# The opening of a two-layer transformer kernel: four phases against one stage with hand-ordered engines

## The reference, cut to what matters

```python
h, hc = x, ctx
mod  = jnp.split((silu_c  @ w_mod[l] + b_mod[l])[:, None, :], 6, axis=-1)   # 1024 -> 6 x 1024
modc = jnp.split( silu_cc @ w_mod[l] + b_mod[l], 6, axis=-1)
u  = modulate(rmsnorm(h,  g_mix_pre[l]), mod[0],  mod[1])     # x * (1 + scale) + shift
uc = modulate(rmsnorm(hc, g_mix_pre[l]), modc[0], modc[1])
t = mixer_inputs(jnp.split(u  @ w_in, IN_OFFSETS, axis=-1), ...)
s = mixer_inputs(jnp.split(uc @ w_in, IN_OFFSETS, axis=-1), ...)
```

## Time and profile before

| | us |
|---|---|
| median of 3 runs (lowest to highest) | 3320.12 (3318.76 to 3322.37) |
| profiled execution | 3324.58 |
| its span, first to last instruction | 3322.8 |
| TensorE busy in it | 3188.5 (96%) |
| DVE, ACT, GpSimd busy | 1708.6, 1135.9, 208.4 |
| mean granted clock of TensorE | 0.983 |

### The profile page before, as it was taken

The page is one execution under the profiler, slowest core; times in us unless marked ns, Lnnn a source line. Parts: engine busy times, 40 slices in busy tenths (PEclk is TensorE's granted clock), DMA queues, the critical chain, the costliest instruction groups (busy, mean ns, idle before and its releaser), DMA issues. The chain is left out here.

```text
span 3322.8 us, 46746 instructions
## 1 busy us (share of the span) xinstructions
PE 3188.5 (96%) x18520; PEld 2889.8 (87%) x18520; DVE 1708.6 (51%) x3172; ACT 1135.9 (34%) x1931; POOL 208.4 (6%) x170
## 2 busy tenths in 40 slices
PE   7999999999999999899999999999999999899999
PEld 4999988998899789899999988887887787788887
DVE  6644445424357865664222475545534478555333
ACT  3223334433322544221222432334433325442223
POOL 0001100100021011000000000110100110100000
PEclk8999999999999999899999989999999999989999
DMA  6511320231052123442221443141221421443333
GB/s 207 174 39 58 83 95 27 77 102 39 26 184 77 39 73 125 133 127 65 69 63 52 142 151 108 60 127 39 99 79 39 159 89 39 140 140 99 106 86 103
DMA packets 352211, 310.42 MB, mean 93 GB/s; under 512 B 40510, under 2 KB 329228, under 8 KB 350604
## 3 DMA queue, kind: packets, MB, share of 16 engines
q1 hardware_dynamic: 330894, 240.65, 24.1%
q10 hardware_dynamic: 21118, 67.03, 5.5%
HBM read 273.94 MB, written 33.29 MB: 92 GB/s over the span
## 5 line engine op out<-in xcount | busy, mean ns | idle before, releaser
L923 PE MATMUL ps<-u_hi,w_hi 128*128 128x384 f32 (+1 forms) x2080 | 602.3, 352 | 25.0 <-DVE u_lo L2521 8.5
L923 PE MATMUL ps<-u_lo,w_hi 128*128 128x384 f32 (+1 forms) x2080 | 596.6, 349 | 0.0
L923 PE MATMUL ps<-u_hi,w_lo 128*128 128x384 f32 (+1 forms) x2080 | 596.6, 349 | 0.0
L2133 DVE TENSOR_TENSOR w_lo<-w_raw,w_hi 128x2048 fp32r<-128x2048 f32 x129 | 297.4, 2305 | 359.5 <-ACT w_hi L1586 357.7
L923 PEld LDWEIGHTS ps<-u_hi,w_hi 128*128 128x128 f32 x2080 | 379.0, 189 | 48.0 <-issue 22.0
L923 PEld LDWEIGHTS ps<-u_hi,w_lo 128*128 128x128 f32 x2080 | 382.3, 189 | 18.8
L923 PEld LDWEIGHTS ps<-u_lo,w_hi 128*128 128x128 f32 x2080 | 382.0, 189 | 18.3
L1586 ACT ACTIVATE w_hi<-w_raw 128x2048 fp32r<-128x2048 f32 x129 | 246.1, 1908 | 198.2 <-issue 90.3
L1301 PE MATMUL ps<-u_hi,w_hi 128*128 128x384 f32 (+1 forms) x816 | 306.1, 375 | 5.9 <-ACT space L1895 3.8
L1301 PE MATMUL ps<-u_hi,w_lo 128*128 128x384 f32 (+1 forms) x816 | 296.5, 363 | 0.0
L1301 PE MATMUL ps<-u_lo,w_hi 128*128 128x384 f32 (+1 forms) x816 | 293.9, 360 | 0.0
(11 more groups left out here) (303 smaller groups left out, 5153.8 us busy)
## 6 DMA issues: line engine op xcount, KB each, us to landing
w_raw<-in_w_in SPq DMA_DIRECT2D x288, 256.0 KB, 4.1
space<-in_w_mod SPq DMA_DIRECT2D x48, 1024.0 KB, 5.4
w_raw<-in_w_gate_up SPq DMA_DIRECT2D x176, 256.0 KB, 4.1
w_raw<-in_w_down SPq DMA_DIRECT2D x114, 192.0 KB, 2.9
w_raw<-in_w_branch SPq DMA_DIRECT2D x64, 256.0 KB, 3.5
w_raw<-in_w_out SPq DMA_DIRECT2D x48, 256.0 KB, 3.7
m_scratch<-space ACTq DMA_DIRECT2D x3, 3072.0 KB, 9.8
space<-m_scratch ACTq DMA_DIRECT2D x3, 3072.0 KB, 10.4
```

Of the source, the lines that this page charges most:

```text
L923: last = nc.tensor.matmul(ps[:, 2 * (t % 2) + b, 0:a1 - a0], wv[w][:, k, j * P:(j + 1) * P], xx[:, k, a0:a1], start=(k == 0 and w == 0 and ...
L2133: V.tensor_tensor(w_lo[slot][:, :], w_raw[slot][:, :], w_hi[slot][:, :].bitcast(F32), ALU.subtract).then_inc(w_lo_done, 1)
```

## The change

The four opening phases become one phase, `opening`, in which each engine has a list of its own and no meeting stands until its end; TensorE counts itself out (`end_products`) before its last two chunks.

- SP: the tokens come first, then the modulation units in the order 0, 4, 1, 5, 2, 6, 3, 7, each as two DMAs; `w_raw0` stands after unit 1; then layer 1's vectors, `w_raw1` and the small broadcasts. The first background units now wait for the store of the tokens (`h_stored`) too.
- ACT squares the tokens token-major from `x_tok` with `accum_out`, so the sums of squares come without DVE and TensorE; it copies the lower half of each turned token tile, DVE the upper.
- DVE scales all eight chunks by the spread root into `first_x` as soon as the root is there; the gain is no longer in it. A pair of modulation units (p and p + 4) gives shift and gain of two chunks (`pair`), and with them ACT finishes a chunk (`chunk`: two Identity passes with scale and bias, then `u_hi`).
- The low part is made by DVE for chunks 0, 2, 4, 6, 7 and by GpSimd for 1, 3, 5.
- The products with the first weight unit (`first_chunk`) are interleaved with the modulation products. `MOD_DVE` is now (5, 6).
- The store of the tokens moves from the head of `norm_mix` to the end of ACT's list; the two rope tables are loaded in the opening. The lambda factors (`head_factors`) move behind it, into the `gemm` phase.

The tables, the plan and SP's list:

```diff
-MOD_DVE = (2, 4)
-MOD_PE = (0, 1, 3, 5, 6, 7)
+MOD_LOADS = (0, 4, 1, 5, 2, 6, 3, 7)
+MOD_DVE = (5, 6)
+MOD_PE = (0, 4, 1, 2, 3, 7)
...
-    phases = [("setup", 0, None), ("load_x", 0, None), ("mod", 0, None)]
+    phases = []
...
-            phases.append(("norm_mix", l, None))
+            phases.append(("opening", l, None))
...
+            for i in MOD_LOADS:
+                for j in range(2):
+                    sp.dma_start(mod_ring[i].rearrange("p (k n) -> p k n", k=KD)[:, 4 * j:4 * j + 4, :],
+                                 mod_cols(0, i * 256)[:, 4 * j:4 * j + 4, :]).then_inc(mod_landed[i], 16)
+                if i == 1:
+                    load_unit(groups_in_order[0], 0, 0)
             load_vectors(sp, 1)
+            load_unit(groups_in_order[1], 0, 0)
...
-                            if phases[index - 1][0] == "close":
+                            if phases[index - 1][0] in ("opening", "close"):
                                 sp.wait_ge(h_stored, 16 * stored)
```

TensorE's list:

```diff
+            def opening(g):
+
+                pe.wait_ge(consts_made, 1)
+                for t in range(NT):
+                    turn_tokens(t)
+                    if t == 4:
+                        turn_vectors(0)
+                pe.wait_ge(scalars_in, 1)
+                mod_product(0, 0)
+                first_roots()
+                mod_product(0, 1)
+                mod_product(1, 0)
+                mod_columns(0, 0)
+                mod_product(1, 1)
+                mod_product(2, 0)
+                mod_columns(1, 0)
+                mod_product(2, 1)
+                mod_columns(2, 1)
+                first_chunk(g, 0)
+                first_chunk(g, 1)
+                mod_product(3, 0)
+                mod_product(3, 1)
+                summed_columns(0, 1)
+                mod_product(4, 0)
+                mod_columns(3, 2)
+                mod_product(4, 1)
+                mod_product(5, 0)
+                mod_columns(4, 2)
+                mod_product(5, 1)
+                first_chunk(g, 2)
+                summed_columns(1, 2)
+                first_chunk(g, 3)
+                mod_columns(5, 3)
+                turn_vectors(1)
+                first_chunk(g, 4)
+                first_chunk(g, 5)
+                ph.end_products(True)
+                first_chunk(g, 6)
+                first_chunk(g, 7)
```

On ACT a chunk, the squares, the order of its list, and the store with its place before:

```diff
+                def chunk(k):
+                    act.wait_ge(x_scaled, k + 1)
+                    act.wait_ge(pair_made, k // 2 + 1)
+                    for sg, seg in segments(False):
+                        last = A(first_x[:, k, seg], first_x[:, k, seg], ACT.Identity, bias=mod_t[:, 0, k, sg:sg + 1],
+                                 scale=gain[:, 0, 0, k, sg:sg + 1])
+                    last.then_inc(first_full, 1)
+                    act.wait_ge(first_full, k + 1)
+                    A(u_hi[:, k, :], first_x[:, k, :], ACT.Copy).then_inc(first_high, 1)
...
+                    A(token_square, x_tok[:, t, :], ACT.Square, accum_out=mean[:, t:t + 1]).then_inc(tokens_squared, 1)
...
+                row(0)
+                row(1)
+                act.wait_ge(w_landed[0], 64)
+                A(w_hi[0][:, :], w_raw[0][:, :], ACT.Copy).then_inc(w_hi_done, 1)
+                row(2)
+                chunk(0)
+                chunk(1)
+                row(3)
+                chunk(2)
+                chunk(3)
+                row(4)
+                row(5)
...
+                chunk(4)
+                chunk(5)
+                chunk(6)
+                split(following, 0, 0)
+                chunk(7)
+                act.wait_ge(vec_turned, 2)
+                A(vec[:, 1, :], ps[:, 4, 0:N_ROWS], ACT.Copy).then_inc(vec_copied, 1)
+                act.dma_start(h_dram[:, :, :], space[:, 8:16, :]).then_inc(h_stored, 16)
...
-                act.dma_start(h_dram[:, :, :], space[:, 8:16, :]).then_inc(h_stored, 16)
```

On DVE the scaling behind the spread root and what follows it, and GpSimd's low parts:

```diff
+                for k in range(KD):
+                    V.tensor_tensor(two(first_x[:, k, :], False), tile_at(8 + k, False), ps[:, 6:8, 0:TOK // 2],
+                                    ALU.mult).then_inc(x_scaled, 1)
+                dve.wait_ge(vec_copied, 1)
+                pair(0, 2)
+                dve.wait_ge(w_hi_done, 1)
+                V.tensor_tensor(w_lo[0][:, :], w_raw[0][:, :], w_hi[0][:, :].bitcast(F32),
+                                ALU.subtract).then_inc(w_lo_done, 1)
+                low(0)
+                sums(0)
+                pair(1, 4)
+                sums(1, 2)
+                pair(2, 7)
+                pair(3, 8)
+                low(4)
+                low(6)
+                split(following, 0, 0)
+                dve.wait_ge(first_low[1], 3)
+                low(7)
+                scalars()
...
+                    for k in (1, 3, 5):
+                        pool.wait_ge(first_high, k + 1)
+                        G.tensor_tensor(u_lo[:, k, :], first_x[:, k, :], u_hi[:, k, :].bitcast(F32),
+                                        ALU.subtract).then_inc(first_low[1], 1)
```

More of the change, by code:

```diff
@@ L564, in norm_spec @@
         def norm_spec(kind, l):
-            if kind == "norm_mix":
-                return [(list(range(8, 16)), KD, False, lambda k, s: gain[:, l, 0, k, s:s + 1],
-                         lambda k, s: mod_t[:, l, k, s:s + 1], (u_hi, u_lo), FFN_SCR)]
             return [(list(range(0, 8)), KD, True, None, None, 8, FFN_SCR)]
@@ L889, in mod_product @@
+            def mod_product(at, half):
+                i = MOD_PE[at]
+                if half == 0 and at < 3:
+                    pe.wait_ge(x_copied[at % 2], NT - 1 + at // 2)
+                if half == 0 and at > 3:
+                    pe.wait_ge(x_scaled, KD)
+                pe.wait_ge(mod_landed[i], 16 * 2)
+                for k in range(4 * half, 4 * half + 4):
+                    last = nc.tensor.matmul(ps[0:2, MOD_BANK[at], 0:256], silu_c[:, k, :],
                                             mod_ring[i][:, k * 256:(k + 1) * 256], start=k == 0, stop=k == KD - 1)
-                last.then_inc(row_ready, 1)
@@ new lines, in summed_columns, with first_chunk @@
+            def summed_columns(at, pair):
+                pe.wait_ge(first_summed, at + 1)
+                pe.wait_ge(pair_made, pair)
+                for j in range(2):
+                    last = part_product(first_part[:, at], j, 4 * MOD_DVE[at], 5)
+                last.then_inc(columns_made, 1)
+            def first_chunk(g, k):
+                if k == 0:
+                    pe.wait_ge(w_lo_done, g.u0 + 1)
+                pe.wait_ge(first_low[k % 2], k // 2 + 1)
+                for j in range(g.nt):
+                    chunk_product(g, g.u0 % 2, g.t0 + j, j, k)
@@ L2258, in prepare_b @@
                 if unit == 2:
+                    if l == 0:
+                        head_factors()
                     dve.wait_ge(lf_log, l + 1)
@@ new lines, in opening, with pair, low, sums @@
+            def opening(following):
+                def pair(p, made):
+                    dve.wait_ge(columns_made, made)
+                    for first in (2 * p, KD + 2 * p):
+                        own.did(V.tensor_tensor(mod_t[:, 0, first:first + 2],
+                                                ps[:, 5, 2 * first:2 * first + 4].rearrange("p (f s) -> p f s", s=2),
+                                                vec[:, 0, first:first + 2].unsqueeze(2).to_broadcast([P, 2, 2]),
+                                                ALU.add))
+                    own.wait()
+                    at = ROWS["g_mix_pre"] + 2 * p
+                    V.scalar_tensor_tensor(gain[:, 0, 0, 2 * p:2 * p + 2], mod_t[:, 0, KD + 2 * p:KD + 2 * p + 2], 1.0,
+                                           vec[:, 0, at:at + 2].unsqueeze(2).to_broadcast([P, 2, 2]), ALU.add,
+                                           ALU.mult).then_inc(pair_made, 1)
+                def low(k):
+                    dve.wait_ge(first_high, k + 1)
+                    V.tensor_tensor(u_lo[:, k, :], first_x[:, k, :], u_hi[:, k, :].bitcast(F32),
+                                    ALU.subtract).then_inc(first_low[k % 2], 1)
+                def sums(at, between=None):
+                    i = MOD_DVE[at]
+                    dve.wait_ge(mod_landed[i], 16 * 2)
+                    for half in range(2):
+                        chunk_sums(first_part[:, at], mod_ring[i], at, range(4 * half, 4 * half + 4))
+                        if half == 0 and between is not None:
+                            low(between)
+                    dve.sem_inc(first_summed, 1)
+                for t in range(NT):
+                    dve.wait_ge(x_turned, 2 * t + 2)
+                    V.tensor_copy(space[:, 12:16, t * P:(t + 1) * P],
+                                  ps[:, 2 * (t % 2) + 1, :].rearrange("p (k n) -> p k n", k=4)).then_inc(x_copied[1], 1)
+                dve.wait_ge(tokens_squared, NT)
+                own.did(V.tensor_scalar(mean[:, :], mean[:, :], 1.0 / D_MODEL, EPS, ALU.mult, ALU.add))
```

(10 more changed lines are left out.)

339 lines of the change are left out of this document (114 added, 225 removed).

## The result

| | before | after |
|---|---|---|
| median of the runs timed side by side (lowest to highest) | 3321.24 (3316.13 to 3324.88) | 3300.79 (3294.46 to 3792.84) |
| ratio, 95% interval | | 0.9934 (0.9919 to 0.9948) |
| profiled execution, its span | 3324.58, 3322.8 | 3302.19, 3300.5 |
| mean granted clock | 0.983 | 0.987 |

The change makes the kernel 0.66% faster, 20 to 22 us, where 10.6 were forecast. (The 3792.84, and two highest values of over 4400 further down, are disturbed runs that the comparisons leave out.) Two more timings of the changed kernel gave 0.9932 and 0.9958, so the gain is 14 to 23 us.

The account below looks back on a forecast made before the run. TensorE is busy 96% of the span, so only its idle time can be won. Unit 2 moves from 109.09 to 94.6, 14.5 us, less 2.4 and 1.5 for clock: gain 10.6, 3320.12 to 3309.5, range 3302 to 3317.

Parts of the forecast that it names:

- Token stage: Opening, loads to spread: 1.9 us a tile on ACT, five tiles end at 15.7, root at 19.6, spread at 20.9.
- handoffs: Token stage on ACT: allowance on top of Square (1.06 us), accumulator read (194 ns) and PSUM copy (594 ns), giving 1.9 a tile.
- From chunk 0 to pair 2: Opening: TensorE starts chunk 0 at 34.3, chunks 0 and 1 end at 41.2 after half clock, pair 2 at 58.2.
- the lock: DVE's second unit of sums: waits for GpSimd's low part of chunk 3 over the shared SBUF ports, charged 1.8 us.
- the store is issued at 69.0: End of ACT's list: from pair 2, chunks 4, 5, 6 (6.3), weight copy 1.9, chunk 7 (2.1), vector copy, then store.
- Behind the store: SP's queue: store lands 8.7 later at 77.7, unit 2's w_lo is ready 16.6 after that, unit 2 begins at 94.6.
- Clock behind unit 2: After TensorE idles 4.3 us ahead of unit 2, half clock costs 1.75 to 2.95 us, taken as 2.4.
- the allowance of 1.5 for one more spell: Token stage, called the weakest part: one more spell of half clock costs nothing to 3.0 us, taken as 1.5.
- DMA is no limit: Opening's loads: modulation units 0, 4, 1 arrive by 19, units 5, 2, 6, 3, 7 and both weights by 42.
- The store doesn't hold the queue up, or the opening ends 5 us sooner: Rival at the opening's end: TensorE's own 17.2 us at unit 1 counts, less clock; time 3303, chance 15%.
- The rivals on the clock: Opening, 3.2 us more per modulation product: ahead of chunk 0, 3316, chance 22%; through the whole opening, 3327, chance 6%.
- GpSimd's lock on the path: Rival in the opening: GpSimd's three low parts hold DVE up for 5.5 us instead of 0.4; 3314.6, chance 9%.

Follow-up runs that it names:

- the one with early weights: Changed kernel with token store issued behind the rope loads and second weight unit's copy and low part ahead of chunks 4 and 6: 3296.97, ratio 0.9935.

## Why the prediction was wrong

The path was the one forecast: store, SP's queue, unit 2's weights, a short idle time, half clock behind it. What was wrong is the size of the steps ahead of the store: the pace of the token stage above all, and the end of ACT's list. All erred to the same side, and with the allowances for the clock they are the miss. Unit 2 was put at 94.6 and stood at 88.28, 6.3 earlier.

- *Token stage*: "Five tiles end at 15.7", the spread at 20.9 and the first product at 34.3. The step that failed is the 1.9 a tile. The durations were right (1.05, 0.19, 0.59), but the "handoffs" were to be taken off, not put on: the copy starts at 10.24 while the accumulator read of 10.15 still runs, and a tile comes each 1.52 (9.21 to 10.72). The root is done at 17.44 for 19.6, and from there to the first `w_in` product 13.9 passed where 14.7 were counted (0.4 of it is the spread: 0.87 for 1.3): at 31.31 it is 3.0 early.
- *From chunk 0 to pair 2*: pair 2 came at 53.3 instead of 58.2, another 1.9. About 1.0 is the half clock in chunks 0 and 1: 3.4 us of it, not 5.9, and product 3 began at 37.23 where 41.2 was forecast. That part is chance, since other profiles had 0 to 6 us there. The rest is small, with the lock at 1.5 (5.17 less 3.62) instead of 1.8.
- *Store*: "the store is issued at 69.0". From pair 2 to there 10.8 were counted and 9.5 passed. Two ACTIVATEs that stand ahead of the store in ACT's list were not over when it was issued (62.74 + 0.85 and 63.50 + 0.24): 1.0 of the 1.3.
- *Behind the store*: right. 8.7 to land, and from there 16.7 to the end of `w_lo` for 16.6; 0.1.
- *Clock behind unit 2*: 1.8 for 2.4, and the allowance of 1.5 for one more spell wasn't needed: 2.1 together. The 2.4 was a fair figure: two more profiles of the kernel had 2.7. With the 6.3 above, 8.4: the forecast 10.6 becomes 19.0, which is what the marks of the first profile show (18.8; 18.1 and 17.1 in the others).
- *"DMA is no limit"* held, but only as a property of the new list. The forecast named the list in one clause and looked for the gain in the stage. With the old list the same stage gains nothing.

Of the rivals, none came whole. "The store doesn't hold the queue up, or the opening ends 5 us sooner" has both halves in one: the opening did end 5 sooner (67.17 for 72.1), and the store still held the queue. The rivals on the clock put 3.2 on a modulation product at half clock; no row shows that figure. The product in the earlier trace rows cost 2.6 more, half a product in the run with the old list 1.7 more (3.57 for 1.89), so 3.4 a whole one. GpSimd's lock on the path did not cost 5.5: it stretched each unit of sums by 1.5, TensorE's weight loads waited 0.36 for the second, where 0.4 was forecast, and the kernel without it was no faster in its one run. The range was too narrow below: allowances for clock and handoffs had been put in on one side only, and the first rival was given the time of unit 1 alone.

What stays open: how much of 14 to 23 us is the true mean. The opening gives 17 to 19 in each profile against the one profile of the kernel before, and about 3 less where that one's half clock is taken for chance; executions differ by 5 and more behind it.

## What to carry to other kernels

Where a stage starts on parts instead of on the whole, order the load queue by the first consumer's need, and check it by running the new stage with the old list: here all of the 20 us went with the new list, and interleaving the products carried none of it while another wait stood behind it. Ask of each store that is moved to a stage's end which load waits for it: here it cost about 5 us, which one moved line gives back. Where a gain is a few us, take more than one profile of each kernel before a step is priced from it: the half clock alone moved the same mark by 1 to 3 us. Where an engine's list of short operations is costed, take the pace from start to start, not the sum of durations with an allowance on top.

## What the runs showed of the hardware

- The same idle time of 2.87 us ahead of chunk 0 was followed by different spells of half clock in kernels that are alike up to there, and in one and the same kernel. The changed kernel had 3.4, 3.4 and 5.3 us in its three profiles, the one with the store early none and 2.9, the one with early weights some 6. The windows of that last one:

```profile
31.00:33.00 2.00, 1.84 (x6) 1.87 (x7) 1.93 (x6) 1.07 (x2) 0.82 (x1) 0.50 1.09 347
...
35.00:37.00 2.00, 2.00 (x8) 2.00 (x7) 1.86 (x5) 0.00 (x0) 0.00 (x0) 0.50 1.09 348
```

  and of the one with the store early, in its first and in its second profile:

```profile
31.00:33.00 2.00, 1.84 (x11) 1.87 (x12) 1.93 (x6) 1.07 (x2) 0.82 (x1) 1.00 1.09 348
...
33.00:35.00 2.00, 2.00 (x10) 2.00 (x9) 1.97 (x3) 0.00 (x0) 1.15 (x1) 0.73 1.09 348
```

- ACT's queue issued a DMA (62.75) while one ACTIVATE ahead of it had just begun (62.74) and another had not (63.50); it waited for neither.
- With the broadcasts in the middle of the list, the twelve of them held SP's queue for 7.1 us, about 0.43 to 0.54 for each but one of 1.72, while near their end the DMA engines moved 34 GB/s (window 28 to 30).
